# Leaving 32 of 256 tokens out of the dense first expert pass and computing their chosen experts by gathered rows

## What is computed

```python
q = (h @ w_q).reshape(b, s, PEER_HEADS, 2, PEER_HALF)          # 8 heads
s1, s2 = scores of both halves against 128 keys each
v1, i1 = lax.top_k(s1, 16);  v2, i2 = lax.top_k(s2, 16)
cand_sc = v1[..., :, None] + v2[..., None, :]                   # 256 candidates
top_sc, pos = lax.top_k(cand_sc, 16)
ids = take_along_axis(i1 * 128 + i2, pos)
g = softmax(top_sc)
u = take(expert_u, ids);  act = gelu(einsum('ced,cd->ce', u, h))
out = einsum('ce,ced->cd', g * act, take(expert_v, ids))
```

## Time and profile before

| what | value |
|---|---|
| median of 3 runs | 3693.86 us (3693.47 to 3694.22) |
| span of the profiled execution | 3691.7 us |
| TensorE busy | 3666.4 us (99%) |
| VectorE, ScalarE, GpSimd busy | 2159.2, 1673.3, 1435.9 us |
| first expert passes | 2 x 128 tiles |
| DMA | 825.51 MB, mean 224 GB/s |

### The profile page before, as it was taken

One profiled execution on the slowest core, in us unless ns is written; L12 is line 12 of the kernel. 1 busy time (PEld: TensorE's weight loads), 2 busy tenths in 40 slices (PEclk: granted clock), 3 DMA queues, 4 the chain that ended last, 5 costly groups with the idle time before them and its releaser, 6 DMA issues.

```text
span 3691.7 us, 47266 instructions
## 1 busy us (share of the span) xinstructions
PE 3666.4 (99%) x19072; PEld 3148.9 (85%) x19072; DVE 2159.2 (58%) x3076; ACT 1673.3 (45%) x2032; POOL 1435.9 (39%) x791
## 2 busy tenths in 40 slices
PE   8999999999999999999999999999999999999998
PEld 7888888888888888888889888888888888888887
DVE  5565799666666444444456558966666654444444
ACT  4365444444444444444455544444444444444444
POOL 2211344777882222222212124478788312222221
PEclk9999999999999999999999999999999999999999
DMA  9844568998777677767754355577777776666674
GB/s 350 277 160 164 190 203 267 261 259 233 216 211 240 245 242 244 243 236 243 245 188 160 121 189 187 210 214 216 209 214 213 216 262 233 247 241 244 233 250 169
DMA packets 255433, 825.51 MB, mean 224 GB/s; under 512 B 88816, under 2 KB 154352, under 8 KB 171760
## 3 DMA queue, kind: packets, MB, share of 16 engines
q1 hardware_dynamic: 128832, 718.38, 56.1%
q10 hardware_dynamic: 52656, 103.82, 7.9%
q0 software_dynamic: 73728, 0.29, 4.4%
HBM read 752.94 MB, written 69.47 MB: 223 GB/s over the span
## 4 chain that ended last, share of the span: by engine, by line
PE 99%; DVE 1%; DMA 0%; ACT 0%; issue 0%; DVEq 0%; SPq 0%; ACTq 0%
PE bank L1503 32%; PE bank L1506 17%; PE bank L1704 12%; PE bank L1708 12%; PE bank L1706 12%; PE bank L1533 3%; PE bank L1535 3%; PE bank L1534 3%; PE bank L1626 0%; PE bank L1607 0%; PE bank L1608 0%; PE bank L1609 0%; PE bank L1874 0%; DVE lo L905 0%; PE bank L1875 0%; PE bank L1567 0%
## 5 line engine op out<-in xcount | busy, mean ns | idle before, releaser
L905 DVE TENSOR_TENSOR lo<-raw,hi 128x1024 fp32r<-128x1024 f32 x1015 | 1253.8, 1236 | 1348.3 <-ACT hi L546 1345.7
L546 ACT ACTIVATE hi<-raw 128x1024 fp32r<-128x1024 f32 x1278 | 1349.8, 1058 | 1339.9 <-PE bank L1708 699.8
L496 POOL TENSOR_TENSOR lo<-raw,hi 128x1024 fp32r<-128x1024 f32 x263 | 634.3, 2412 | 2029.5 <-ACT hi L546 2029.5
L1503 PE MATMUL bank<-act_t,hi 128*128 128x512 f32 x5120 | 1224.4, 391 | 10.7 <-ACT hi L546 9.6
L1503 PEld LDWEIGHTS bank<-act_t,hi 128*128 128x128 f32 x5120 | 941.5, 188 | 193.5 <-issue 9.6
L513 POOL DMA_INDIRECT w_rows<-gate,place_u x512 | 797.3, 1557 | 201.9 <-issue 151.3
L1506 PEld LDWEIGHTS bank<-act_t,lo 128*128 128x128 f32 x5120 | 659.3, 191 | 26.4 <-issue 1.4
L1506 PE MATMUL bank<-act_t,lo 128*128 128x256 f32 x5120 | 673.2, 283 | 1.1 <-DVE lo L905 1.1
L1704 PE MATMUL bank<-hi,wa 128*128 128x512 f32 x2024 | 623.2, 389 | 0.9 <-DVE stage L924 0.9
L1706 PE MATMUL bank<-lo,wa 128*128 128x512 f32 x2024 | 623.1, 389 | 0.0
L1708 PE MATMUL bank<-hi,wa 128*128 128x512 f32 x2024 | 623.0, 389 | 0.0
(11 more groups left out here) (235 smaller groups left out, 1862.7 us busy)
## 6 DMA issues: line engine op xcount, KB each, us to landing
raw<-in_stream SPq DMA_DIRECT2D x647, 1024.0 KB
w_rows<-zeros SPq DMA_DIRECT2D x64, 512.0 KB, 8.7
act_rows<-stage ACTq DMA_DIRECT2D x64, 512.0 KB
acts<-act_rows ACTq DMA_DIRECT2D x64, 512.0 KB, 4.3
w_part<-w_rows ACTq DMA_DIRECT2D x64, 512.0 KB, 5.5
w_rows<-gate,place_u POOLq DMA_INDIRECT x512
xt_in<-in_x_t SPq DMA_DIRECT2D x4, 512.0 KB, 7.9
x_res<-in_x SPq DMA_DIRECT2D x2, 1024.0 KB, 14.4
```

The lines of the kernel that those rows point to most:

```text
L496: pool.tensor_tensor(lo[:, s, :], raw[:, n0 % RAW_SLOTS, j * HALF:(j + 1) * HALF], hi[:, s, :].bitcast(F32), ALU.subtract).then_inc(lo_rea ...
L546: act.activation(hi[:, s, :], half, ACT.Copy).then_inc(hi_ready[s], 1)
L905: dve.tensor_tensor(lo[:, s, :], half, hi[:, s, :].bitcast(F32), ALU.subtract).then_inc(lo_ready[s], 1)
L1503: ins = mm(ps[:], hi[:, s, at], act_t[:, kt, :, :].rearrange("p w t -> p (w t)"), start=(kt == 0), stop=(kt == KT - 1), skip_group_check=True)
```

## The change

The last 32 tokens leave the first expert pass. Its products have 448 and 224 columns instead of 512 and 256, so `stage`, `act_rows` and `w_rows` shrink to 224 tokens. ScalarE copies the second PSUM half to `part`, VectorE adds the first half to it and then scales.

For the 32 tokens the 128 chosen experts each (4096 pairs) are laid out as 32 columns of 128 partitions (four groups of 32 tokens, each with another quarter of a head's 16 places). GpSimd gathers, per column, 128 rows of `peer_u` (8 KB each) by an indirect DMA into one of three buffers; VectorE multiplies them by the normed token rows and sums (`dot`, one in every third tile from tile 9 to 102); ScalarE applies gelu, VectorE multiplies by the gate, and GpSimd scatters the finished coefficients into a second DRAM table (`pair_dram`), which `load_group` reads as the last 32 columns of a group. A gather waits for the dot product three before it.

Routing is done head by head: per head one unit, one unit, one pair and one decode step, the first 16 steps in consecutive laps from lap 2 of the query product, the others one in every five (tiles 2 to 77 of the pass); the softmax of a head follows two laps later. GpSimd takes `lo` halves only until tile 2 of the pass and then deals its work out in 32 rounds: gathers, pair scatters and 8 scatters each, the second group's with 96 rows. Zeros: 32 stores of 4 tiles x 224 tokens and two of the second table per layer.

```diff
+SPARSE = 32
+DENSE = S - SPARSE
+PER_HEAD = TOPK // PAIR_GROUPS
+GATHERS = PEER_HEADS * PER_HEAD
+GATHER_BUFS = 3
+NEAR_STEPS = 16
+STEP_SPREAD = 5
+POOL_UNTIL = 2
+DOT_FIRST, DOT_SPREAD = 9, 3
...
+def step_unit(k):
+    return ROUTE_AT + (k if k < NEAR_STEPS else NEAR_STEPS + STEP_SPREAD * (k - NEAR_STEPS))
+ROUTE_STEPS = {step_unit(k): divmod(k, 4) for k in range(4 * PEER_HEADS)}
+EXPS = {step_unit(4 * h + 2) + 1: h for h in range(PEER_HEADS)}
+GATES = {step_unit(4 * h + 3) + 1: h for h in range(PEER_HEADS)}
+PAIR_COPIES = {step_unit(4 * h + 3) + 2: h for h in range(PEER_HEADS)}
+DOTS = {DOT_FIRST + DOT_SPREAD * j: j for j in range(GATHERS)}
...
+def gathers_in(q):
+    return [j for j in range(GATHERS) if 3 * j // 4 == q]
+def pair_heads_in(q):
+    return [h for h in range(PEER_HEADS) if 5 + 13 * h // 4 == q]
...
+            def gather(layer, j):
+                pool.wait_ge(pairs_ready, layer * PEER_HEADS + j // PER_HEAD + 1)
+                if j >= GATHER_BUFS:
+                    pool.wait_ge(dots_done, layer * GATHERS + j - GATHER_BUFS + 1)
+                pool.indirect_dma_start(pair_rows[j % GATHER_BUFS][:], None, u_rows[layer],
+                                        bass.IndirectOffsetOnAxis(ap=pair_u[:, 1, j:j + 1], axis=0)).then_inc(
+                                            gathered[j % GATHER_BUFS], 16)
...
             def scatter(layer):
                 pool.wait_ge(zeroed[layer], 16 * ZERO_STORES)
-                pool.wait_ge(sel_ready, layer + 1)
+                pool.wait_ge(normed_in, 16 * (PAIR_GROUPS - 1) * (layer + 1))
+                pool.wait_ge(c_free, GRANTED + C0[f"wq{layer}"] + PEER_HEADS)
                 rows = w_dram[layer].rearrange("i p t -> (i p t)").unsqueeze(1)
+                for q in range(GATHERS):
+                    h, i = divmod(q, PER_HEAD)
+                    for j in gathers_in(q):
+                        gather(layer, j)
+                    for late in pair_heads_in(q):
+                        scatter_pairs(layer, late)
+                    if i == 0:
+                        pool.wait_ge(sel_ready, layer * PEER_HEADS + h + 1)
+                        if h >= 1:
+                            pool.wait_ge(scattered[h - 1], 16 * NC_TOK * TOPK * (layer + 1))
+                    for c, rows_of in enumerate((P, FIRST_SPARSE)):
+                        for k in range(TOPK * h + 4 * i, TOPK * h + 4 * i + 4):
+                            pool.indirect_dma_start(
+                                rows, bass.IndirectOffsetOnAxis(ap=place_u[0:rows_of, c, k:k + 1], axis=0),
+                                gate[0:rows_of, c, k:k + 1], None, compute_op=ALU.add).then_inc(scattered[h], 16)
...
                 if g == 0:
                     for h in range(PEER_HEADS):
                         act.wait_ge(scattered[h], 16 * NC_TOK * TOPK * (layer + 1))
+                    act.wait_ge(pair_scattered, 16 * GATHERS * (layer + 1))
...
+                def copy_part(t):
+                    unit_done(act, base + t)
+                    if t >= 2:
+                        act.wait_ge(a_free, GRANTED + a0 + t - 1)
+                    act.activation(part[:, t % 2, :], ps_a[(a0 + t) % 2][:, DENSE:2 * DENSE], ACT.Copy).then_inc(
+                        part_ready, 1)
...
-                    scaled_sum(stage[:, t % STAGED, :], a0 + t, ps_b[1])
+                    dve.wait_ge(part_ready, layer * TILES + t + 1)
+                    st = stage[:, t % STAGED, :]
+                    dve.tensor_tensor(st, ps_a[(a0 + t) % 2][:, 0:DENSE], part[:, t % 2, :], ALU.add).then_inc(a_free, 1)
+                    dve.wait_ge(a_free, GRANTED + a0 + t + 1)
+                    dve.tensor_tensor(st, st, inv_row[:, 0:DENSE], ALU.mult).then_inc(summed, 1)
+
+                def dot(j):
+                    b = j % GATHER_BUFS
+                    uses = len(range(b, GATHERS, GATHER_BUFS))
+                    dve.wait_ge(gathered[b], 16 * (layer * uses + j // GATHER_BUFS + 1))
+                    if j == 0:
+                        dve.wait_ge(normed_in, 16 * (PAIR_GROUPS - 1) * (layer + 1))
+                    dve.tensor_tensor_reduce(pair_rows[b][:], pair_rows[b][:], normed[:], 1.0, 0.0, ALU.mult, ALU.add,
+                                             pair_dot[:, j:j + 1]).then_inc(dots_done, 1)
...
                         if high:
-                            ins = mm(ps[:], hi[:, s, at], act_t[:, kt, :, :].rearrange("p w t -> p (w t)"),
-                                     start=(kt == 0), stop=(kt == KT - 1), skip_group_check=True)
+                            both = ps[:, 0:2 * tokens].rearrange("p (w t) -> p w t", w=2)
+                            ins = mm(both, hi[:, s, at], act_t[:, kt, :, 0:tokens], start=(kt == 0), stop=(kt == KT - 1),
+                                     skip_group_check=True)
                         else:
-                            ins = mm(ps[:, 0:S], lo[:, s, at], act_t[:, kt, 0, :], start=False, stop=False,
+                            ins = mm(ps[:, 0:tokens], lo[:, s, at], act_t[:, kt, 0, 0:tokens], start=False, stop=False,
                                      skip_group_check=True)
```

More of the change, by code:

```diff
@@ L410, in gpsimd_takes @@
                 return s % 2 == 1
-            busy = any(U0[f"wq{k}"] + LEAD <= n0 < U0[f"peer{k}"] + SCATTER_AT for k in range(2))
+            busy = any(U0[f"wq{k}"] + LEAD <= n0 < U0[f"peer{k}"] + POOL_UNTIL for k in range(2))
             return s % 2 == 1 if busy else s == HALF_SLOTS - 1
@@ L501, in split_range, with load_gain, spread_normed @@
                     split_lo(n)
+            def load_gain(layer):
+                pool.wait_ge(stds, 6 if layer else 2)
+                pool.dma_start(normed[FIRST_SPARSE:P, :], peer_g[layer:layer + 1, :].to_broadcast([SPARSE, D])).then_inc(
+                    gain_in, 16)
+                if layer == 0:
+                    pool.memset(zeros[1][:], 0.0).then_inc(zeros_set, 1)
+            def spread_normed(layer):
+                pool.wait_ge(normed_ready, layer + 1)
+                for g in range(PAIR_GROUPS - 1):
+                    pool.dma_start(normed[SPARSE * g:SPARSE * (g + 1), :], normed[FIRST_SPARSE:P, :]).then_inc(
+                        normed_in, 16)
@@ new lines, in scatter_pairs @@
+            def scatter_pairs(layer, h):
+                pool.wait_ge(pair_weighted, layer * PEER_HEADS + h + 1)
+                if h >= 1:
+                    pool.wait_ge(pair_scattered, 16 * (layer * GATHERS + PER_HEAD * h))
+                rows = pair_dram[layer].rearrange("p i t -> (p i t)").unsqueeze(1)
+                for j in range(PER_HEAD * h, PER_HEAD * (h + 1)):
+                    pool.indirect_dma_start(
+                        rows, bass.IndirectOffsetOnAxis(ap=pair_u[:, 0, j:j + 1], axis=0), pair_coef[:, j:j + 1],
+                        None, compute_op=ALU.add).then_inc(pair_scattered, 16)
@@ new lines, in _ @@
+            pool.iota(ranks[:], pattern=[[1, TOPK]], base=0, channel_multiplier=0,
+                      allow_small_or_imprecise_dtypes=True).then_inc(route_consts, 1)
+            at = 0
+            for layer in range(2):
+                split_range(at, U0[f"wq{layer}"] + 3)
+                load_gain(layer)
+                split_range(U0[f"wq{layer}"] + 3, U0[f"wq{layer}"] + 6)
+                spread_normed(layer)
+                at = U0[f"peer{layer}"] + POOL_UNTIL
+                split_range(U0[f"wq{layer}"] + 6, at)
+                scatter(layer)
@@ new lines, in decode @@
+                at = slice(TOPK * h, TOPK * (h + 1))
+                if (layer, h) == (0, 0):
+                    dve.wait_ge(route_consts, 1)
+                steps.do(dve.tensor_scalar(place_f[:, 0, :], first[:, 0, :], float(NKEYS * DENSE), token[:, 0:1], ALU.mult,
+                                           ALU.add))
+                steps.do(dve.tensor_scalar(place_f[:, 1, :], first[:, 1, :], place_by[:, 1:2], place_by[:, 3:4], ALU.mult,
+                                           ALU.add))
@@ L1183, in peer @@
+            def route_step(layer, i):
+                if i in GATES:
+                    finish_softmax(layer, GATES[i])
+                if i not in ROUTE_STEPS:
+                    return
+                h, r = ROUTE_STEPS[i]
+                if r < 2:
+                    route_unit(layer, 2 * h + r)
+                elif r == 2:
+                    route_pairs(h)
+                    start_softmax(layer, h)
+                else:
+                    decode(layer, h)
             def peer(layer):
```

287 lines of the change are left out of this document (172 added, 115 removed).

## The result

The changed kernel takes 3810.6 us (median, 3808.9 to 3813.0) against 3694.0 (3693.5 to 3695.1): a ratio of 1.0316, 95% interval [1.0302, 1.0331]. I had forecast 3629, faster. It is slower by 117 us, and lies outside the range. The profiled execution has a span of 3808.9 us against 3691.7.

A forecast was written before the change was run, and what follows sets the result against it. TensorE, busy 3666.4 of 3691.7 us, was taken to bound the kernel. Layer 1 gains 44 us, layer 0 27, query phases lose 6: together 65, span 3626.7, so 3629 us as median; range 3572 to 3715.

The forecast's parts named there:

- TensorE: First expert passes: narrower products cut a tile from 5.56 to 5.03 us, 68 us less per layer if nothing else waits.
- Rival 4: TensorE's 224-column products run at the plain float32 rate, 0.39 us instead of 0.12; near 4700 us; chance 0.04.
- GpSimd: First pass: 320 indirect DMAs at 1.857 us, 594 us, plus waits; its list ends at 645 us, making a new wait.
- Gather 31 waits for dot 28: First pass, GpSimd's queue: gather 31 goes only after dot 28, behind tile 93, at 491 us.
- The wait behind the load: Tile 122: gelu and copy queue behind ScalarE's load_group(0); TensorE stops at 639 us, restarts near 650, pass 671.
- VectorE: First pass: work fits on average, 4.5 of 5.03 us a tile; bursts cost about 13 us, 660 a pass.
- rival 5: Dots at half rate, 4.5 us, slow VectorE to some 5.7 us a tile; near 3715 us; chance 0.04.
- The query phase: Query product before each first pass: routing steps in each unit cost 3 us per layer (0 to 8).
- DMA: Layer 0's first pass: engines need 5.83 us per 5.16 us tile in tiles 2 to 70; wait 17 us (0 to 33).
- 44 + 27: Forecast gains of the first passes: layer 1 715 - 671 = 44 us, layer 0 27 after 17 of DMA wait.
- rival 3: First passes: gathers move at half the stream's rate, 6 us of the DMA engines each; slower, 3819 us; chance 0.11.
- rival 2: Hard DMA wall, 33 us in layer 0, up to 10 in layer 1; gathers may hold GpSimd 3 us; 3650-3680; chance 0.18.

The follow-up runs named there:

- Experiment 8: Kernel before, with ScalarE running the gelu of tile j-1 in place of that of tile j in the first pass: 3922.3 us against 3694.6.
- experiment 5: Changed kernel, with ScalarE's gelu of tile j directly after tile j's copy, instead of the gelu of tile j-1 ahead of it: 3766.0 us.
- experiment 3: Changed kernel, with the first pass's products at 512 and 256 columns again: 3848.7 us.
- experiment 7: Changed kernel, VectorE's first-pass lo splits in two pieces with second operand from PSUM (leftover values), dots from tile 4 instead of 9: 3651.1 us.
- Experiment 10: Changed kernel, with one operand of each two-input VectorE routing operation in a PSUM bank instead of SBUF: 3796.1 us.
- experiment 16: Changed kernel, lo splits in two pieces, dots from tile 4, dots' normed rows and heads 0 to 3's routing operands in PSUM: 3643.7 us against 3694.2.
- experiment 9: Changed kernel, with VectorE's first-pass lo splits in two instructions of 512 elements, both operands still in SBUF: 3721.8 us.

## Why the prediction was wrong, by its steps

**TensorE: right.** Sixteen wide products take 3.27 us, 0.204 each, sixteen narrow ones 1.78, 0.111 each, and the undisturbed tile is 5.05 us against my 5.03. Rival 4 falls.

**GpSimd: the failed step.** "320 x 1.857" and "80 x 1.857 = 149". Gather 31 went at 1068.5, 565 us after the pass began at 503.5, where I had 491; the 80 operations behind it took 172.8 us to the last one's start, 2.16 each, where I had 149. Held scatters are the cause of most of it: with the splits cut in two and their second operand in PSUM (experiment 1) gather 31 goes at 1028.6 and an operation behind it takes 1.91. "Gather 31 waits for dot 28" failed too. Dot 28 had ended at 1030.0, 527 us into the pass, and gather 31 stood another 38.5 us behind GpSimd's own older work. So 36 of the 74 us by which it was late are the pace of the tiles, and the rest is GpSimd's queue.

I took a duration from rows in which it hardly varied, passed over the 1.86 in the first of them, and did not ask what kept it steady. Experiment 8 shows that ScalarE's order alone destroys the clear phase. Neither the old order alone (experiment 5, scatters at 1766 ns) nor the old beat alone (experiment 3, 1907 ns) brings it back in the changed kernel.

**The wait behind the load: right in place, wrong in size.** The stop came when tile 122's work queued behind ScalarE's load, released by a scatter's landing, 73.3 and 68.1 us instead of 11. Of the 182 us over my forecast these two stops make 119 (141 against 22), the query stages 23 (29 against 6), and the slower pace of the passes the remaining 40.

**VectorE: durations right, bursts too small.** A dot takes 2.286 us (2.25 forecast), so rival 5 falls. But in experiment 7, where the splits don't hold scatters, tile 0 to 127 takes 675.7 us against 127 x 5.05 = 641: 34 us more. TensorE's waits for VectorE's sums are 24.7 of them, 4.9 of which are the stop behind the load; that leaves some 20 for bursts, where I had 13. Eight key products of 0.44 are another 3.5.

**The query phase: 3 us a layer forecast, 16.3 and 12.5 measured**, outside the 0 to 8 that I gave. Experiment 10 puts 8.8 of layer 0's 16.3 on VectorE waiting for GpSimd's splits.

**DMA: wrong, too dark.** With the scatters free (experiment 7) layer 0's pass takes 675.7 us and layer 1's 676.6: no wait in layer 0, where I took 17. The engines show 1.02 and 328 GB/s in 640 to 860 (350 in the highest slice of the earlier trace rows). The Trainium skill ("DMA: Bandwidth & Descriptors", Where 436 GB/s comes from) gives one core about 358 GB/s of HBM; by that this wait was near 0, and the runs agree.

**The sum.** In experiment 7 the span is 42.4 us shorter than before although the stretches ahead of the first tiles are 28 longer: from tile 0 to 127 the passes gain 34.3 and 35.2, together 69.5, close to the 44 + 27 that I had, but by errors that cancel, which is luck: some 31 us too little for the tiles' pace in both layers together, 17 too much for DMA and some 6 a layer too much for the stop behind the load. So the mechanism of the gain was right, and what was not in the sum is the holding of GpSimd's scatters.

**The rivals.** 3811 lies by rival 3's 3819, but that wasn't it: dots waited for gathers only 37.4 us in both layers together, and without any gathers the kernel still took 3757 (experiment 2). None of my rivals was the cause. The nearest was the aside in rival 2 of an indirect DMA that holds GpSimd longer; I gave it to the 32 gathers alone and not to the 256 scatters.

## What to carry to other kernels

A duration that is nearly the same in every row may come from a phase, the place of one engine's work in another's beat, and not be a price: look at the few rows that differ and at what runs beside them, and ask whether the change moves that. Before GpSimd gets more to do, set its indirect DMAs against VectorE's instructions with two SBUF operands; keep one of these operands in a free PSUM bank, or cut the instruction in two; together with earlier dots these made 3643.7 us of 3810.6 (experiment 16). And when a line moves on an engine with time to spare, ask whose start its wait had been setting: one such line cost the kernel before 228 us, and was worth 45 in the changed one.

## What the runs showed of the hardware

- An indirect DMA on GpSimd takes 1.43 us for 96 rows and 1.55 for 128, with 0.30 of issue, while VectorE is idle. One that starts inside a VectorE instruction with two SBUF inputs, earlier than some 0.14 us before its end, ends 1.30 or 1.43 after that instruction's end; with the second input in PSUM it isn't held (255 scatters, 1496 ns). One that starts inside the first 0.035 us of such an instruction wasn't always held.
- The reverse: a VectorE match of 1.22 us takes 3.30 beside a GpSimd split.
- Two pieces back to back let the waiting GpSimd in after the first of them (102 of 104 scatters, experiment 9); a gap made by a semaphore adds nothing to that.
- The DMA engines read 1.01 to 1.02 at 325 to 328 GB/s over 220 us with TensorE busy for 96 to 97% of them.
- In a stretch of 70 us in which TensorE is busy for 10.8 the granted clock reads 0.54; before, busy for all 70, it reads 1.00.
